# WKV stage: keys and values in one half of the partitions, beta and u in the other, and tiles turned whole

## The reference

```
def step(S, inp):
    r_t, w_t, k_t, v_t, kk_t, a_t = inp
    sa = jnp.einsum('bhvk,bhk->bhv', S, kk_t)
    S = (S * w_t[:, :, None, :]
         - sa[..., None] * (kk_t * a_t)[:, :, None, :]
         + v_t[..., None] * k_t[:, :, None, :])
    y = jnp.einsum('bhvk,bhk->bhv', S, r_t)
    return S, y
```

## Time and profile before

| | us |
|---|---|
| median of 3 runs (2235.35 to 2236.99) | 2235.78 |
| profiled execution, own time | 2238.37 |
| its span, first to last instruction | 2236.6 |
| TensorE busy in the span | 2171.8 |
| DVE busy | 1480.1 |
| ACT busy | 1074.0 |

### The profile page before, as it was taken

How to read it: one execution, slowest core, us unless ns; L and a number is a source line. 1 busy time by engine, 2 the same in 40 slices (tenths; PEclk the granted TensorE clock), 3 DMA queues, 4 the chain that set the end, 5 groups by cost and what they waited for, 6 DMA issues and landing times.

```text
span 2236.6 us, 40207 instructions
## 1 busy us (share of the span) xinstructions
PE 2171.8 (97%) x15616; PEld 1863.0 (83%) x15616; DVE 1480.1 (66%) x2054; ACT 1074.0 (48%) x1508; POOL 88.7 (4%) x78
## 2 busy tenths in 40 slices
PE   9999999999999999999899999998799999999997
PEld 7888888888888888888788878887788888888886
DVE  6656568885588856885874689773476644566655
ACT  5444564444444434445544755433334534456533
POOL 0700000000000000000000000002110000000000
PEclk9999999999999999999999999999999999999998
DMA  8654545555555555555465555652344555654552
GB/s 291 208 161 152 171 151 178 188 188 188 188 188 188 187 188 188 188 168 191 138 217 142 176 159 162 210 160 67 99 165 155 171 186 188 190 155 145 168 180 85
DMA packets 402744, 383.93 MB, mean 172 GB/s; under 512 B 43505, under 2 KB 401393, under 8 KB 401777
## 3 DMA queue, kind: packets, MB, share of 16 engines
q1 hardware_dynamic: 402610, 382.05, 53.9%
HBM read 374.65 MB, written 7.34 MB: 171 GB/s over the span
## 4 chain that ended last, share of the span: by engine, by line
PE 87%; DVE 8%; issue 2%; ACT 2%; DMA 1%; SPq 0%; DVEq 0%; ACTq 0%
PE acc L775 45%; PE acc L778 22%; PE acc L806 3%; PE aux L1141 2%; PE acc L861 2%; PE acc L862 2%; PE acc L863 2%; DVE w_lo L1986 2%; PE acc L809 2%; PE acc L1141 1%; PE aux L1056 1%; PE aux L878 1%; ACT w_hi L1372 1%; PE aux L1076 1%; DVE inverse L2422 0%
## 5 line engine op out<-in xcount | busy, mean ns | idle before, releaser
L1986 DVE TENSOR_TENSOR w_lo<-raw_w,w_hi 128x1024 fp32r<-128x1024 f32 (+1 forms) x592 | 714.1, 1225 | 457.1 <-ACT w_hi L1372 455.5
L1372 ACT ACTIVATE w_hi<-raw_w 128x1024 fp32r<-128x1024 f32 (+1 forms) x592 | 613.5, 1046 | 674.3 <-PE acc L778 575.1
L775 PE MATMUL acc<-h,w_hi 128*128 128x512 f32 x1664 | 525.9, 397 | 1.2 <-DVE w_lo L1986 1.2
L778 PEld LDWEIGHTS acc<-h,w_lo 128*128 128x128 f32 x1664 | 312.6, 188 | 73.8
L778 PE MATMUL acc<-h,w_lo 128*128 128x256 f32 x1664 | 327.0, 278 | 0.0
L775 PEld LDWEIGHTS acc<-h,w_hi 128*128 128x128 f32 x1664 | 254.5, 189 | 2.2 <-issue 1.4
L775 PE MATMUL acc<-x_split,w_hi 128*128 128x512 f32 x704 | 225.2, 401 | 0.0
L775 PE MATMUL acc<-ff,w_hi 128*128 128x512 f32 x704 | 221.7, 396 | 2.4 <-DVE ff L2243 2.4
L775 PE MATMUL acc<-xs_b,w_hi 128*128 128x512 f32 x512 | 162.5, 399 | 1.7 <-DVE w_lo L2431 0.9
L778 PEld LDWEIGHTS acc<-ff,w_lo 128*128 128x128 f32 x704 | 132.2, 188 | 31.3
L778 PEld LDWEIGHTS acc<-x_split,w_lo 128*128 128x128 f32 x704 | 132.2, 188 | 31.2
(11 more groups left out here) (373 smaller groups left out, 3138.3 us busy)
## 6 DMA issues: line engine op xcount, KB each, us to landing
raw_w<-in_w_up SPq DMA_DIRECT2D x176, 512.0 KB, 3.5
raw_w<-in_a_w_in SPq DMA_DIRECT2D x128, 512.0 KB, 3.3
raw_w<-in_w_in SPq DMA_DIRECT2D x64, 512.0 KB, 4.3
raw_w<-in_w_down SPq DMA_DIRECT2D x64, 512.0 KB, 3.2
raw_w<-in_b_w_qg SPq DMA_DIRECT2D x64, 512.0 KB, 3.8
raw_w<-in_w_o SPq DMA_DIRECT2D x32, 512.0 KB, 3.3
raw_w<-in_a_w_out SPq DMA_DIRECT2D x32, 512.0 KB, 3.3
raw_w<-in_w_k_shared SPq DMA_DIRECT2D x32, 512.0 KB, 4.0
```

The costliest lines, as they stand in the source:

```text
L775: pe.matmul(ACC[2 * b + f], WHI[:, q, k, f * P:(f + 1) * P], op[:, kt, :, :].rearrange("p h t -> p (h t)"), start=first, stop=False)
L778: mm = pe.matmul(ACC[2 * b + f][:, 0:T], WLO[:, slot, k, f * P:(f + 1) * P], op[:, kt, 0, :], start=False, stop=last)
L1372: act.activation(WHI[:, u % 4, 0:ku, :], RAWW[:, u, 0:ku, :], ACT.Copy).then_inc(hi_made, 1)
L1986: dve.tensor_tensor(WLO[:, u, 0:ku, :], RAWW[:, u, 0:ku, :], WHI[:, u % 4, 0:ku, :].bitcast(F32), ALU.subtract)\
```

## The change

- The two terms of the state product become one product over 128 partitions. `k_and_beta` holds, for each tile, k in one half of the partitions and beta in the other; `v_and_u` holds v in the half of k and u in the half of beta. The output product is the same with `with_rho`, where the masked k-by-r and beta-by-r pairs lie in the two halves. Each becomes eight matmuls with 128 rows.
- The tiles are turned whole: a matmul takes 128 channels of a tile (both heads) against the 128x128 identity or centring matrix. There are four for v, four for k and four for beta; k and beta are turned only where c < 3.
- ScalarE copies v in two pieces of 64 partitions, and k with beta in one piece of 128x512.
- The final u is copied half by ScalarE and half by VectorE. VectorE's copy stands right after its add to x, ahead of the group norm's work.
- `quads` gets a rule (`channel`, `between`, `across`) for the half and the bank of the result, and the halves of AKK, u and the cross blocks are laid out anew (`tok`, `far`, `mid`).
- The output product of a step is one group after `x_first(n + 1)`; before, half of it was ahead of it.
- VectorE masks in two operations instead of three.
- SP loads the cross blocks in four DMAs instead of two. The bonus rows and the norm's rows are stored by four DMAs each instead of one, with the four tiles' rows of one head side by side in DRAM.
- Two semaphores of the setup become one (`ones_set`).

```diff
-            def quads(banks, at, n, lhs, rhs, from_tok, to_tok, start, stop):
+            channel, between = (lambda h_, e: (h_, e)), (lambda h_, e: (h_ ^ e, e))
+            across = lambda h_, e: (1 - e, h_)
+
+            def quads(banks, at, lhs, rhs, place, start, stop):
                 for j in range(2):
                     for e in range(2):
-                        for h_ in ((1, 0) if e and from_tok and to_tok else (0, 1)):
-                            b = h_ ^ e if to_tok else h_
-                            mm = pe.matmul(banks[64 * b:64 * b + 64, e, at + j * n:at + (j + 1) * n], lhs(h_, 2 * j + e), rhs(h_, 2 * j + e),
+                        for h_ in range(2):
+                            b, bank = place(h_, e)
+                            mm = pe.matmul(banks[64 * b:64 * b + 64, bank, at + j * CHUNK:at + (j + 1) * CHUNK], lhs(h_, 2 * j + e), rhs(h_, 2 * j + e),
                                            start=(start and j == 0), stop=(stop and j == 1))
...
+            vu = lambda m: lambda h_, i: v_and_u(m)[:, i // 2, i % 2, h_, :]
+            kb = lambda m: lambda h_, i: k_and_beta(m)[:, i * P + h_ * CHUNK:i * P + (h_ + 1) * CHUNK]
+            rho = lambda m: lambda h_, i: with_rho(m)[:, h_, i, :]
...
             def turns(n):
...
-                quads(TOK_BANKS, 0, CHUNK, at(V, n), centre, False, True, True, False)
-                quads(TOK_BANKS, P, CHUNK, at(BET, n), one, False, True, False, False)
-                quads(TOK_BANKS, T, CHUNK, at(K, n), one, False, True, False, True).then_inc(tok_done, 1)
+                for i in range(4):
+                    b = i % 2
+                    mm = pe.matmul(TOK_BANKS[64 * b:64 * b + 64, 1, i // 2 * P:(i // 2 + 1) * P], tile(V, i), CENTRE, start=(i < 2), stop=(i >= 2))
+                if c < 3:
+                    if n:
+                        pe.wait_ge(kb_out, k_beta_turned(n - 1))
+                    for i in range(4):
+                        b = i % 2
+                        pe.matmul(TOK_BANKS[64 * b:64 * b + 64, 0, i * P:(i + 1) * P], tile(K, i), IDENT, start=(i < 2), stop=False)
+                    for i in range(4):
+                        b = 1 - i % 2
+                        mm = pe.matmul(TOK_BANKS[64 * b:64 * b + 64, 0, i * P:(i + 1) * P], tile(BET, i), IDENT, start=False, stop=(i >= 2))
+                mm.then_inc(tok_done, 1)
...
-                    quads(PAIR_BANKS, 384, CHUNK, tok_kind(m, K_TOK), tok_kind(m, V_TOK), True, False, True, False)
                 if c == 0 and g:
                     pe.wait_ge(gn_read, g)
-                pe.wait_ge(rest_out, n + 1)
-                quads(Y_BANKS, 0, CHUNK, tok_kind(m, V_TOK), tok(small(m, ARK)), True, False, c == 0, False)
-                pe.wait_ge(us_ready, 2 * n + 2)
+                pe.wait_ge(us_ready, 3 * n + 3)
                 if c < 3:
-                    quads(PAIR_BANKS, 384, CHUNK, tok_kind(m, BET_TOK), tok(US), True, False, False, True).then_inc(s_done, 1)
+                    quads(PAIR_BANKS, 384, kb(m), vu(m), channel, True, True).then_inc(s_done, 1)
                 if more:
                     x_first(n + 1)
-                quads(Y_BANKS, 0, CHUNK, tok(US), tok(small(m, ARB)), True, False, False, True).then_inc(y_done, 1)
+                quads(Y_BANKS, 0, vu(m), rho(m), channel, c == 0, True).then_inc(y_done, 1)
...
                 act.wait_ge(tok_done, n + 1)
-                for a, b in ((0, P), (P, 384)):
-                    act.activation(in_token_halves(n % 2)[:, :, a:b], TOK_BANKS[:, :, a:b], ACT.Copy).then_inc(tok_out, 1)
+                for e in range(2):
+                    act.activation(v_and_u(m)[64 * e:64 * e + 64, :, e, :, :],
+                                   TOK_BANKS[64 * e:64 * e + 64, 1, 0:T].rearrange("p (j h t) -> p j h t", j=2, h=2), ACT.Copy).then_inc(vt_out, 1)
+                if n % NCH < 3:
+                    act.activation(k_and_beta(m), TOK_BANKS[:, 0, :], ACT.Copy).then_inc(kb_out, 1)
...
-                act.activation(in_slots(US), by_two(XU_BANKS[:, :, P:T]), ACT.Copy).then_inc(us_ready, 1)
+                act.activation(v_and_u(n % 2)[0:64, :, 1, :, :].rearrange("p j h t -> p h j t"), by_two(XU_BANKS[0:64, :, P:T]), ACT.Copy)\
+                   .then_inc(us_ready, 1)
...
                 dve.tensor_tensor(slots(XS), by_two(XU_BANKS[:, :, T:384]), slots(XS), ALU.add).then_inc(ws_ready, 1)
+                dve.wait_ge(u_done, 2 * n + 2)
+                dve.tensor_copy(v_and_u(n % 2)[64:P, :, 0, :, :].rearrange("p j h t -> p h j t"), by_two(XU_BANKS[64:P, :, P:T])).then_inc(us_ready, 1)
                 if c == 0 and g:
...
-                for hh in range(2):
-                    sp.dma_start(CRS[64 * hh:64 * hh + H, m, :, H:], cross[c, hh, 2, :, 4 * g:4 * g + 4, :]).then_inc(t_loaded[m], 16)
+                for e in range(2):
+                    for h_ in range(2):
+                        sp.dma_start(CRS[64 * (1 - e):64 * (1 - e) + H, m, 2 * h_:2 * h_ + 2, H:], cross[c, h_ ^ e, 2, :, 4 * g + e:4 * g + 4:2, :])\
+                          .then_inc(t_loaded[m], 16)
...
-                sp.dma_start(g_dram[g], GROWS[:, 1, :]).then_inc(gn_stored, 16)
-                sp.wait_ge(gn_stored, 16 * (g + 1))
+                for i in range(4):
+                    sp.dma_start(g_dram[g, :, i, :], GROWS[32 * i:32 * i + 2, 1, :]).then_inc(gn_stored, 16)
+                sp.wait_ge(gn_stored, 64 * (g + 1))
```

More of the change, by code:

```diff
@@ L450, in program, with k_kappa, with_rho, v_and_u @@
         lt_dram, t_dram, x_dram = dram("lt_scratch", (P, 3, H, H)), dram("t_scratch", (P, 2, H, H)), dram("x_scratch", (P, KD, T))
[L451 to L461, removed]
+        g_dram, b_dram = dram("head_rstd_scratch", (3, 2, 4, T)), dram("bonus_scratch", (8, 4, T))
+        def k_kappa(m):
+            return SMALL[:, m, 0, :].rearrange("p (i c) -> p i c", i=4)
+        def with_rho(m):
+            return SMALL[:, m, 1:3, :].rearrange("p h (i t) -> p h i t", i=4)
+        def v_and_u(m):
+            return SMALL[:, m, 3:5, :].rearrange("p a b -> p (a b)").rearrange("p (j e h t) -> p j e h t", j=2, e=2, h=2)
+        def k_and_beta(m):
+            return SMALL[:, m, 5:7, :].rearrange("p a b -> p (a b)")
+        def k_beta_turned(n):
+            g, c = STEPS[n]
+            return 3 * g + min(c, 2) + 1
         PAIR_BANKS, TOK_BANKS = BANKS[:, 0:2, :], BANKS[:, 2:4, :]
@@ L1180, in pairs @@
                         pe.wait_ge(s_taken, 3 * gp + cp)
-                quads(PAIR_BANKS, 0, P, at(K, n), rho_kappa, False, True, True, False)
-                quads(PAIR_BANKS, T, CHUNK, at(BET, n), at(R, n), False, True, False, True).then_inc(prep_done, 1)
+                for i in range(4):
+                    e, j = i % 2, i // 2
+                    a, apart = i * CHUNK, T + j * CHUNK - i * CHUNK
+                    for h_ in range(2):
+                        both = PAIR_BANKS[64 * e:64 * e + 64, h_, a:a + 2 * apart].rearrange("p (x s) -> p x s", x=2)[:, :, 0:CHUNK]
+                        pe.matmul(both, part(K, h_, 4 * g + i, c), RK[64 * h_:64 * h_ + 64, :, 4 * g + i, c * CHUNK:(c + 1) * CHUNK],
+                                  start=(j == 0), stop=False)
@@ L1184, in turns @@
+                for i in range(4):
+                    b, a = 1 - i % 2, i * CHUNK
+                    for h_ in range(2):
+                        mm = pe.matmul(PAIR_BANKS[64 * b:64 * b + 64, h_, a:a + CHUNK], part(BET, h_, 4 * g + i, c), part(R, h_, 4 * g + i, c),
+                                       start=False, stop=(i >= 2))
+                mm.then_inc(prep_done, 1)
             def turns(n):
-                one = lambda h_, i: IDENT[64 * h_:64 * h_ + 64, 64 * h_:64 * h_ + 64]
-                centre = lambda h_, i: CENTRE[64 * h_:64 * h_ + 64, 64 * h_:64 * h_ + 64]
+                g, c = STEPS[n]
@@ L1218, in last_rows_wide @@
                         mm.then_inc(gn_wide, 1)
-            V_TOK, BET_TOK, K_TOK = range(3)
             def x_first(n):
@@ L1232, in x_second @@
                 pe.wait_ge(s_ready, 3 * g + c)
-                quads(XU_BANKS, 0, CHUNK, at(KAP, n), state, False, True, False, True).then_inc(x_done, 1)
+                quads(XU_BANKS, 0, at(KAP, n), state, between, False, True).then_inc(x_done, 1)
             def step(n):
@@ L1238, in step @@
                 more = n + 1 < len(STEPS)
-                inverse, cross = block_of(TB[:, n % 3, :, :]), block_of(CRS[:, n % 3, :, :])
+                inverse, cross = block_of(TB[:, n % 3, :, :]), far(CRS[:, n % 3, :, :])
                 if c > 0:
@@ L1249, in step @@
                 if c > 0:
-                    quads(Y_BANKS, 0, CHUNK, state, at(R, n), False, False, True, False).then_inc(s_read, 1)
-                pe.wait_ge(us_ready, 2 * n + 1)
-                quads(XU_BANKS, T, CHUNK, cross, tok(US), True, True, True, True).then_inc(w_done, 1)
+                    quads(Y_BANKS, 0, state, at(R, n), channel, True, False).then_inc(s_read, 1)
+                pe.wait_ge(us_ready, 3 * n + 1)
```

(1 more changed line is left out.)

77 lines of the change are left out of this document (44 added, 33 removed).

## The result

| us | before | after |
|---|---|---|
| median (7 runs each) | 2235.35 | 2241.09 |
| lowest to highest | 2230.85 to 2236.99 | 2240.02 to 2244.81 |
| profiled execution, own time | 2238.37 | 2244.81 |
| its span | 2236.6 | 2243.0 |
| the stage of the recurrence | 120.06 | 124.80 |

The ratio is 1.0031, 95% interval [1.002, 1.0041]: slower by 5.7 us of the medians, where 2.5 us less was forecast. The time lies just above the forecast's range.

A forecast was written before the change was run, and what follows sets the result against it. The stage's chain between three engines was taken to run near its instruction supply's pace. Stage 114.9 against 120.1, 5.2 less, plus 1.5 late instructions and 1.2 low clock: net 2.5 less, 2233.3 us; range 2224 to 2241.

The forecast's parts named there:

- low clock: TensorE's clock falls to 1.2 GHz around long waits; one dip, in c=1, adds 1.2 us to the sum.
- late instructions: TensorE's remaining supply waits in the stage, for transfers late behind other loads: 1.5 us, where 14.0 stood.
- c=1 8.6 three times: Steps of chunk 1 in the three later groups: 8.6 us each, with the reciprocal displaced behind VectorE's new copy.
- first group: The four steps, chunks c=0 to 3, of group g=0: 6.6, 6.7, 5.9 and 5.9 us.
- c = 2, three steps: Steps of chunk 2 in the later groups: 6.5 us each, the weight split delaying the decay by 0.6.
- Chain of a step: u to cross 0.96 us, cross to second u product 1.83, that to S 1.10 and to x_second 2.83.
- Supply: In the stage, 1344 matmuls instead of 1792: 21 instruction packets instead of 28, supply waits under 4 us.
- Rival 3: The stage's 14.0 us of TensorE waits aren't for instructions and stay: 12 us more, 2248; chance 0.08.
- VectorE's order: VectorE's new copy of u displaces group-norm work onto the chain; in later c=1 steps x_first 3.80 us after u2.
- Steps that end on `x_first`: For c=3, x_first starts 1.60 us after the second u product; the next u comes 1.55 later.
- Rival 1: VectorE's displaced work finds gaps and every supply wait in the stage goes: gain 10 to 15 us; chance 0.20.
- Rival 2: Shape changes at turns and S cost 0.15 us more each: net 8 us more, 2244; chance 0.12.

The follow-up runs named there:

- e2: Kernel after plus eight products of constants ahead of `x_first` in steps 5, 9 and 13, filling TensorE's gap: 2240.26 us, ratio 1.0005.
- e5: Kernel after with VectorE's norm work and weight splits behind the decay, scaling before u's copy, root behind ScalarE's first u copy in c = 2: 2228.84 us, ratio 0.9963.
- e8: Kernel after with only the reciprocal moved behind the state's decay, and the root to c = 2 behind the first copy of u: 2235.85 us, ratio 0.9992.
- e1: Kernel after with VectorE's norm work and weight splits behind the decay, scaling before u's copy, root in c = 2 ahead of ScalarE's first u copy: 2232.34 us.
- e9: Kernel after with scaling ahead of u's copy, weight splits and head products behind the decay, reciprocal and root left in place: 2240.87 us, ratio 1.0012.
- e6: Kernel before with group-norm work and weight splits behind the decay, root behind ScalarE's first copy of u in c = 2: 2236.61 us, ratio 0.9998.
- e4: Kernel after with ScalarE copying both halves of the final u and VectorE's copy removed: 2244.53 us, ratio 1.0032.
- e3: Kernel after with turns as 64x64 parts in four corners, twelve matmuls more per step of chunks 0 to 2, four in chunk 3: 2243.98 us, ratio 1.0032.
- e7: e5 with the turns of e3, the two diffs together: 2233.16 us, ratio 0.9983.

## Why the prediction was wrong
Its working of the chain held. Its failed step is the low clock: it put 1.2 us for one dip in "To it come 1.5 of late instructions and 1.2 of low clock (one dip: the longest idle, about 2.2 us, is now in c=1)". The idle time was right (2.22 us). But it stands in three steps, as the prediction's own "c=1 8.6 three times" has it, and the clock fell in all three: 4.6 us by e2, three dips of 1.54. The other terms of the sum were each off by less.

Point by point, forecast and measured in the stage:

| us | before | forecast | after |
|---|---|---|---|
| start, end | 3.45, 5.49 | 4.0, 5.3 | 4.39, 5.36 |
| first group, four steps | 26.83 | 25.1 | 26.50 |
| c = 0, three steps | 24.02 | 23.4 | 24.10 |
| c = 1, three steps | 22.83 | 25.8 | 31.00 |
| c = 2, three steps | 24.01 | 19.5 | 19.91 |
| c = 3, two steps | 13.44 | 11.8 | 13.54 |
| late instructions and low clock, on top | in the rows | 2.7 | in the rows |
| stage | 120.06 | 117.6 | 124.80 |

Against the kernel before, the c = 2 steps give 4.1 us and the c = 1 steps take 8.2.

- **Chain of a step: right.** u to cross 0.96 us (0.96 forecast), cross to u 1.85 (1.83), u to S 1.10 (1.10), u to `x_second` in step 2 2.85 (2.83). The first three are in the rows of step 5. The turns cost 0.44 to 0.48 each for 0.43.
- **Supply: right.** 21 packets (21), waits of 2.1 us (under 4, and 1.5 in the sum). Rival 3, that the waits stay, is refuted: they follow the instructions. Over the kernels of this study the stage has 2736 or 2737 records and 2.1 to 4.8 us of waits, 3056 records and 8.6 or 9.9, about 3635 and 14.0 or 14.5. That these waits are for instructions is an inference from this and from the packets.
- **VectorE's order: right in kind.** The reciprocal was to make `x_first` come 3.80 us after u; it came 4.00. e2, e5 and e8 give its price without the low clock as 2.08 us per step, and the prediction had 8.6 less about 6.7, 1.9. The scaling and the head products in c = 0 cost 0.57 to 0.92: these steps take 7.80, 8.15 and 8.15, and 7.23 in e5.
- **Low clock: mis-sized, the step that failed.** 4.6 us in the c = 1 steps by e2, for 1.2 in the sum: 3.4 of the 7.2 us that the stage was off, and more than the 2.5 us of gain. With 4.6 in its place the sum says 0.9 us slower, so this term turns the sign; the other 3.8 us are the smaller misses in this list.
- **Steps that end on `x_first`: short by 0.2 to 0.4.** From `x_first` on to u the prediction took 1.55 us; in step 3 it took 1.91 (1536.37 to 1538.28) and in step 11 1.73, since `x_first` with the output product needs 1.13 to 1.20 and not 0.82. Together with a start of `x_first` 0.12 later this is 0.5 in step 3 and 0.3 in step 11. Most of the rest of the c = 3 and of the first group's excess is waits for instructions, in steps 2 and 7, for which the 1.5 us had been put by.
- **Rival 1, the supply was everything: half right, elsewhere.** In the change's own order it fails. In e5's order the stage falls by 8.7 us against before, near the 10 us at which this rival began, and the gain shows that VectorE's displaced work can find gaps, once it stands behind the decay. (By its own terms the prediction's chances sum to 0.35 for faster by more and 0.20 for slower, not 0.36 and 0.19; nothing hangs on it.)
- **Rival 2, shape changes: refuted.** They cost 0.14 (cross to V turn 0.39 less 0.25), as the prediction took, not 0.15 more.
- **Net, an estimate from the profiled executions.** Without its 14.0 us of supply waits and some 3.5 of low clock the stage before is 102.6 us; e5's, without its 3.5 of waits, 107.8. So the whole turns, products in one piece and split copies together lengthen the chain by 5.2. To that come in the kernel after 2.1 of supply waits, 6.2 for the reciprocal, 4.6 for the clock behind it, and 2.4 in the c = 0 steps: 123.1 of the 124.80 measured, with 1.7 not assigned.

What stays open: the long wait for instructions in step 7. It is there in e1, e5, e8 and e9 (1.36 to 2.46 us) and in e6, the kernel before in the new order (3.29), and shorter in e4 and after (1.12 and 0.81). In e8 the 256 KB spreads of the norm's rows are issued at 1557.99, and the only instruction packets between 1555 and 1566 start at 1560.98 and 1564.46. That these loads hold up the packets is an inference; no run took them away. Also open is why e8's median lies 3 us above the expected range: its one profiled execution has the long step 7, and whether the others have it is not known. And open is what decides whether the clock falls: the length of the one wait ahead of it does not, by the rows of e2 and e3.

## What to carry to other kernels
When a change puts a new operation on a queue, everything behind it in that queue moves to the new place with it: go through what stood beside other work there and put it behind the last operation of the chain, before the change is judged. A gap on TensorE is to be priced with the clock that may follow it, once for every step that has it: here 2.1 us for the reciprocal and 1.5 for the clock. And where the instruction supply is near the pace of the stage, count instructions first: twelve more products a step cost as much as the array time that they saved (e3) or more (e7).

## What the runs showed of the hardware
- The supply turns from nearly free to costly over a small range: in a stage of 111 to 126 us, 21 or 22 packets of 16 KB come with 1.8 to 4.8 us of waits, 24 with 8.6 to 9.9, 28 with 14.0 to 14.5.
- A full-height group of eight products with 64 columns takes 0.62 us from start to start with its change of shape (e8, step 5: 1550.50 to 1551.12), a turn of four with 128 columns 0.44 to 0.48 (after, step 5), and the same turn as eight 64x64 products on four corners 0.24 (e3, step 5), though that is twice the matmuls.
- In seven of the eight idle stretches of 2.2 us on TensorE (three in the kernel after, three in e9, two in e3) the clock fell in or just behind the stretch, for 3.4 or 6.8 us; in step 9 of e3 it did not. Of e4's four waits of 1.8 us two had low clock behind them. In e5, with a wait of 0.64 us in most steps and none above 1.4 between the first and the last of the stage, it stayed at the upper level. Eight products of constants in the gap took the low clock away in steps 5, 9 and 13 at no cost in time (e2), though it then fell once in step 11.
